# Down projections of a two-layer trunk: the block sums of the activations made one pair at a time, in place, eight units ahead; one weight sum written over the loaded block

## What is computed

```python
D_MODEL = 2048; SEQ = 256; DEPTH = 2
D_FF = 11 * D_MODEL // 4                     # 5632

def conv_glu_ffn(h, w_up, conv_w, conv_b, w_down):
    gu = h @ w_up
    gate, up = jnp.split(gu, 2, axis=-1)
    gate = causal_depthwise_conv(gate, conv_w, conv_b)
    return (jax.nn.silu(gate) * up) @ w_down

def reference(x, ...):
    for i in range(DEPTH):
        ...                                   # token mixer
        h = rms_norm(x, ffn_norm[i])
        x = x + conv_glu_ffn(h, ffn_w_up[i], ffn_conv_w[i], ffn_conv_b[i], ffn_w_down[i])
    return x
```

## Time and profile before

| | |
|---|---|
| median of 3 runs | 2106.0 us |
| lowest and highest | 2105.87 and 2107.36 us |
| the profiled execution | 2106.89 us, of which 2105.1 us is the span of the trace |
| mean granted TensorE clock | 0.997 of full |
| down stage of layer 0, from its first matmul | 893.61 us of the span |
| down stage of layer 1, from its first matmul | 1861.41 us of the span |
| busy, of the span | PE 99%, PEld 84%, DVE 67%, ACT 50%, POOL 0% |

### The profile page before, as it was taken

The page is one execution under the profiler, slowest core; times in us unless marked ns, Lnnn a source line. Parts: engine busy times, 40 slices in busy tenths (PEclk is TensorE's granted clock), DMA queues, the critical chain, the costliest instruction groups (busy, mean ns, idle before and its releaser), DMA issues.

```text
span 2105.1 us, 29925 instructions
## 1 busy us (share of the span) xinstructions
PE 2085.9 (99%) x10866; PEld 1778.5 (84%) x10866; DVE 1419.4 (67%) x1692; ACT 1048.1 (50%) x1353; POOL 0.7 (0%) x5
## 2 busy tenths in 40 slices
PE   9999999999999999999999999999999999999999
PEld 8888888888888888878888877888888888878887
DVE  5664565566676676686885677566676666687884
ACT  6554554544444444444554666554444444444553
POOL 0000000000000000000000000000000000000000
PEclk9999999999999999999999999999999999999999
DMA  7665555655655565556666544565565565556665
GB/s 251 208 180 170 165 176 172 188 173 186 191 192 185 189 199 176 189 171 203 201 208 184 181 145 135 179 185 171 194 198 173 188 198 195 178 164 210 194 210 167
DMA packets 206266, 390.69 MB, mean 186 GB/s; under 512 B 12860, under 2 KB 17772, under 8 KB 206188
## 3 DMA queue, kind: packets, MB, share of 16 engines
q1 hardware_dynamic: 203884, 387.45, 58.2%
q10 hardware_dynamic: 2304, 2.20, 0.3%
HBM read 387.48 MB, written 2.11 MB: 185 GB/s over the span
## 4 chain that ended last, share of the span: by engine, by line
PE 93%; DVE 4%; ACT 1%; DMA 1%; issue 1%; DVEq 0%; ACTq 0%
PE ps L1301 39%; PE ps L1291 31%; PE ps L1297 16%; PE ps L1316 2%; PE ps L1318 2%; PE ps L1317 2%; DVE wlo L946 1%; PE ps L1439 1%; DMA raw<-in_ffn_w_down 1%; DVE tlo L944 0%; ACT thi L658 0%; PE ps L1491 0%; PE ps L1502 0%; PE ps L1519 0%; DVE xf L1029 0%
## 5 line engine op out<-in xcount | busy, mean ns | idle before, releaser
L1291 PE MATMUL ps<-hs,whi 128*128 128x512 f32 x2832 | 663.6, 390 | 0.0
L1291 PEld LDWEIGHTS ps<-hs,whi 128*128 128x128 f32 x2832 | 524.7, 188 | 104.3
L990 DVE TENSOR_TENSOR wlo<-raw,whi 128x1024 fp32r<-128x1024 f32 x352 | 414.5, 1220 | 288.2 <-PE ps L1297 202.8
L946 DVE TENSOR_TENSOR wlo<-raw,whi 128x1024 fp32r<-128x1024 f32 x352 | 426.1, 1222 | 255.9 <-ACT whi L660 254.9
L660 ACT ACTIVATE whi<-raw 128x1024 fp32r<-128x1024 f32 x354 | 373.3, 1059 | 373.6 <-PE ps L1301 325.1
L667 ACT ACTIVATE whi<-raw 128x1024 fp32r<-128x1024 f32 x352 | 366.0, 1056 | 265.3 <-DMA raw<-in_ffn_w_up 201.6
L1297 PEld LDWEIGHTS ps<-hs,wlo 128*128 128x128 f32 x2816 | 352.6, 191 | 8.8
L1297 PE MATMUL ps<-hs,wlo 128*128 128x256 f32 x2816 | 355.3, 283 | 0.0
L1301 PE MATMUL ps<-whi,hs 128*128 128x512 f32 x1088 | 276.4, 396 | 0.7 <-ACT whi L660 0.7
L1301 PE MATMUL ps<-whi,gs 128*128 128x512 f32 x1024 | 257.2, 393 | 3.2 <-ACT whi L660 3.2
L1301 PEld LDWEIGHTS ps<-whi,hs 128*128 128x128 f32 x1088 | 199.9, 188 | 40.9 <-DVE hs L1012 0.9
(11 more groups left out here) (194 smaller groups left out, 1394.9 us busy)
## 6 DMA issues: line engine op xcount, KB each, us to landing
raw<-in_ffn_w_up SPq DMA_DIRECT2D x352, 512.0 KB, 4.5
raw<-in_ffn_w_down SPq DMA_DIRECT2D x176, 512.0 KB, 4.6
raw<-in_fox_w_in SPq DMA_DIRECT2D x98, 512.0 KB, 3.9
raw<-in_swa_w_in SPq DMA_DIRECT2D x40, 512.0 KB, 3.6
raw<-in_fox_w_out SPq DMA_DIRECT2D x32, 512.0 KB, 3.8
raw<-in_swa_w_out SPq DMA_DIRECT2D x32, 512.0 KB, 3.8
xk<-in_x SPq DMA_DIRECT2D x8, 256.0 KB, 5.9
out_x<-xk SPq DMA_DIRECT2D x8, 256.0 KB, 4.8
```

The costliest lines, as they stand in the source:

```text
L946: tt(wlo[slot][:, :], raw[slot][:, :], whi[slot][:, :].bitcast(F32), ALU.subtract).then_inc(lo_ready, 1)
L990: tt(wlo[slot][:, :], raw[slot][:, :], whi[slot][:, :].bitcast(F32), ALU.subtract).then_inc(lo_ready, 1)
L1291: return pe.matmul(ps[:, bank, :], whi[slot][:, c:c + P], moving.rearrange("p h t -> p (h t)"), start=first, stop=last)
```

## The change

`tsum`, `thi` and `tlo` hold three sums instead of four. The sum B12+B22 is written over B12 in the "t" slot, and the whole "t" slot is then split as for any other unit, after the sums; the product that uses it moves ahead of the wait for `thi` and `tlo`. The activations' sums are made for one pair at a time, in a buffer of four blocks that lies over `sqj`, each in place of what it was made from: "xc" eight places ahead of the pair (place 1 for the first), "xs" two places after that. The number of matmuls stays.

```diff
@@ -103,6 +103,7 @@
 LAST_OF = [max(i for i, s in enumerate(DOWN_ORDER) if s[:2] == ("d", g)) for g in range(4)]
+FIRST_SEVEN = [DOWN_ORDER.index(("s", 0, k)) for k in SEVEN_K]
 LAST_SEVEN = [max(i for i, s in enumerate(DOWN_ORDER) if s[:2] == ("t", c)) for c in range(2)]
...
@@ -175,12 +177,11 @@
         tsum_at = hs_at + SEVEN * 3 * 2 * P * 4
-        tsum = sb("tsum", [P, 4, 512], at=tsum_at)
-        thi = sb("thi", [P, 4, 512], F32R, at=tsum_at + 8192)
-        tlo = sb("tlo", [P, 4, 512], F32R, at=tsum_at + 16384)
-        xf = sb("xf", [P, SEVEN, 2, T], at=tsum_at)
-        xc = sb("xc", [P, SEVEN, 4, P], at=tsum_at + SEVEN * 2 * T * 4)
-        assert tsum_at + 24576 <= place[0]
+        tsum = sb("tsum", [P, 3, 512], at=tsum_at)
+        thi = sb("thi", [P, 3, 512], F32R, at=tsum_at + 6144)
+        tlo = sb("tlo", [P, 3, 512], F32R, at=tsum_at + 12288)
+        xf = sb("xf", [P, 4, P], at=sqj_at)
+        assert tsum_at + 18432 <= place[0]
         place[0] += -place[0] % 512
...
@@ -474,7 +474,9 @@
                 u = base + i
-                steps += {0: [("xf", layer)], 1: [("xc", layer)], 2: [("xs", layer)]}.get(i, [])
+                for r in range(SEVEN):
+                    at = i - max(1, FIRST_SEVEN[r] - 8)
+                    steps += {0: [("xc", layer, r)], 2: [("xs", layer, r)]}.get(at, [])
                 for c in range(2):
...
@@ -651,13 +653,13 @@
                 if kind == "t":
-                    act.activation(whi[slot][:, 512:1024], raw[slot][:, 512:1024], ACT.Copy).then_inc(hi_ready, 1)
                     act.wait_ge(v_t, 4 * m + 4)
+                act.activation(whi[slot][:, :], raw[slot][:, :], ACT.Copy).then_inc(hi_ready, 1)
+                if kind == "t":
+                    act.wait_ge(v_glo, UP_GROUPS * (m // (2 * SEVEN) + 1) + 1)
                     if m:
                         act.wait_ge(v_tl, m)
                     act.activation(thi[:, :, :], tsum[:, :, :], ACT.Copy).then_inc(a_th, 1)
-                    return
-                act.activation(whi[slot][:, :], raw[slot][:, :], ACT.Copy).then_inc(hi_ready, 1)
 
...
@@ -677,6 +679,8 @@
                     act.wait_ge(f_rd, 2 * FOX_GROUPS)
+                if n == 2:
+                    act.wait_ge(v_xs, SEVEN)
                 for t in range(TT):
...
@@ -715,9 +719,10 @@
                 elif kind == "xs":
-                    act.wait_ge(v_xc, 4 * n + 4)
-                    act.activation(xs[:, :, :, 0, :], xc[:, :, 0:3, :], ACT.Copy)
-                    act.activation(gs[:, 0:SEVEN, 0, 0, P:T], xc[:, :, 3, :], ACT.Copy).then_inc(a_xh, 1)
+                    act.wait_ge(unit_done, U_FFN[n] + 16 * UP_GROUPS)
+                    act.wait_ge(v_xc, 5 * (SEVEN * n + s[2] + 1))
+                    act.activation(xs[:, s[2], :, 0, :], xf[:, 0:3, :], ACT.Copy)
+                    act.activation(gs[:, s[2], 0, 0, P:T], xf[:, 3, :], ACT.Copy).then_inc(a_xh, 1)
                 elif kind == "rcol":
...
@@ -937,13 +942,10 @@
                     seven_sums(u, m)
+                tt(wlo[slot][:, :], raw[slot][:, :], whi[slot][:, :].bitcast(F32), ALU.subtract).then_inc(lo_ready, 1)
                 if kind == "t":
-                    half = slice(512, 1024)
-                    tt(wlo[slot][:, half], raw[slot][:, half], whi[slot][:, half].bitcast(F32), ALU.subtract).then_inc(lo_ready, 1)
                     dve.wait_ge(a_th, m + 1)
                     tt(tlo[:, :, :], tsum[:, :, :], thi[:, :, :].bitcast(F32), ALU.subtract).then_inc(v_tl, 1)
-                    return
-                tt(wlo[slot][:, :], raw[slot][:, :], whi[slot][:, :].bitcast(F32), ALU.subtract).then_inc(lo_ready, 1)
 
...
@@ -952,15 +954,18 @@
                 dve.wait_ge(w_land[(u + 1) % RAW], 16 * ((u + 1) // RAW + 1))
+                if m % (2 * SEVEN) == 0:
+                    dve.wait_ge(unit_done, U_FFN[m // (2 * SEVEN)] + 16 * UP_GROUPS)
+                    dve.wait_ge(v_glo, UP_GROUPS * (m // (2 * SEVEN) + 1) + 1)
                 if m:
                     dve.wait_ge(v_tl, m)
                     dve.wait_ge(v_e, 7 * (m // SEVEN))
                 tt(tsum[:, 0, :], b11, b12, ALU.add).then_inc(v_t, 1)
-                tt(tsum[:, 1, :], b12, b22, ALU.add).then_inc(v_t, 1)
                 dve.wait_ge(v_t, 4 * m + 1)
-                tt(tsum[:, 2, :], tsum[:, 0, :], b22, ALU.add).then_inc(v_t, 1)
+                tt(b12, b12, b22, ALU.add).then_inc(v_t, 1)
+                tt(tsum[:, 1, :], tsum[:, 0, :], b22, ALU.add).then_inc(v_t, 1)
                 dve.wait_ge(v_t, 4 * m + 3)
-                tt(tsum[:, 3, :], tsum[:, 2, :], b21, ALU.add).then_inc(v_t, 1)
+                tt(tsum[:, 2, :], tsum[:, 1, :], b21, ALU.add).then_inc(v_t, 1)
 
...
@@ -1022,25 +1027,27 @@
                     seven_out(n, s[2], s[3], s[4])
-                elif kind == "xf":
-                    dve.wait_ge(unit_done, U_FFN[n] + 16 * UP_GROUPS)
-                    dve.wait_ge(v_glo, UP_GROUPS * (n + 1) + 1)
-                    part = lambda h: gs[:, 0:SEVEN, 0:2, h, :].bitcast(F32)
-                    tt(xf[:, :, :, :], part(0), part(1), ALU.add).then_inc(v_xf, 1)
                 elif kind == "xc":
-                    a11, a21, a12, a22 = (xf[:, :, f, t * P:t * P + P] for f in range(2) for t in range(TT))
-                    n1, s3, s4, s1 = (xc[:, :, i, :] for i in range(4))
-                    dve.wait_ge(v_xf, n + 1)
-                    tt(s1, a21, a22, ALU.subtract).then_inc(v_xc, 1)
-                    tt(s3, a11, a21, ALU.subtract).then_inc(v_xc, 1)
-                    dve.wait_ge(v_xc, 4 * n + 1)
-                    tt(n1, a11, s1, ALU.subtract).then_inc(v_xc, 1)
-                    dve.wait_ge(v_xc, 4 * n + 3)
-                    tt(s4, a12, n1, ALU.subtract).then_inc(v_xc, 1)
+                    x0, e0 = SEVEN * n + s[2], 5 * (SEVEN * n + s[2])
+                    n1, s3, s4, s1 = (xf[:, i, :] for i in range(4))
+                    part = lambda h: gs[:, s[2], 0:2, h, :].bitcast(F32)
+                    dve.wait_ge(v_glo, UP_GROUPS * n + s[2] + 2)
+                    dve.wait_ge(a_ss, 8 * n + 8)
+                    if x0:
+                        dve.wait_ge(v_xs, x0)
+                    tt(xf[:, :, :].rearrange("p (f t) c -> p f (t c)", t=TT), part(0), part(1), ALU.add).then_inc(v_xc, 1)
+                    dve.wait_ge(v_xc, e0 + 1)
+                    tt(s1, s3, s1, ALU.subtract).then_inc(v_xc, 1)
+                    dve.wait_ge(v_xc, e0 + 2)
+                    tt(s3, n1, s3, ALU.subtract).then_inc(v_xc, 1)
+                    dve.wait_ge(v_xc, e0 + 3)
+                    tt(n1, n1, s1, ALU.subtract).then_inc(v_xc, 1)
+                    dve.wait_ge(v_xc, e0 + 4)
+                    tt(s4, s4, n1, ALU.subtract).then_inc(v_xc, 1)
                 elif kind == "xs":
-                    dve.wait_ge(a_xh, n + 1)
-                    tt(xs[:, :, :, 1, :], xc[:, :, 0:3, :], xs[:, :, :, 0, :].bitcast(F32), ALU.subtract)
-                    tt(gs[:, 0:SEVEN, 0, 1, P:T], xc[:, :, 3, :], gs[:, 0:SEVEN, 0, 0, P:T].bitcast(F32), ALU.subtract).then_inc(v_xs, 1)
+                    dve.wait_ge(a_xh, SEVEN * n + s[2] + 1)
+                    tt(xs[:, s[2], :, 1, :], xf[:, 0:3, :], xs[:, s[2], :, 0, :].bitcast(F32), ALU.subtract)
+                    tt(gs[:, s[2], 0, 1, P:T], xf[:, 3, :], gs[:, s[2], 0, 0, P:T].bitcast(F32), ALU.subtract).then_inc(v_xs, 1)
                 elif kind == "prep":
...
@@ -1320,8 +1327,9 @@
                 if kind == "s":
+                    if c == 0:
+                        pe.wait_ge(v_xs, SEVEN * layer + i + 1)
                     if first:
-                        pe.wait_ge(v_xs, layer + 1)
                         pe.wait_ge(v_up, UP_GROUPS * (layer + 1) + 1)
...
@@ -1329,12 +1337,12 @@
                 product(2, mixed(2), w(whi, 1), w(wlo, 1), False, False)
+                product(7, mixed(1), w(whi, 0), w(wlo, 0), first, last)
                 pe.wait_ge(a_th, m + 1)
                 pe.wait_ge(v_tl, m + 1)
                 product(5, act_in(0, 1), sums(thi, 0), sums(tlo, 0), first, last)
-                product(7, mixed(1), sums(thi, 1), sums(tlo, 1), first, last)
-                product(6, mixed(0), sums(thi, 2), sums(tlo, 2), first, last)
-                product(1, act_in(1, 1), sums(thi, 3), sums(tlo, 3), False, False).then_inc(unit_done, 1)
+                product(6, mixed(0), sums(thi, 1), sums(tlo, 1), first, last)
+                product(1, act_in(1, 1), sums(thi, 2), sums(tlo, 2), False, False).then_inc(unit_done, 1)
 
...
```

More of the change, by code:

```diff
@@ L165, in trunk @@
         ssum = sb("ssum", [P, TT])
+        sqj_at = place[0]
         sqj = sb("sqj", [P, TT, 512])
@@ L352, in trunk @@
         v_out = sem("v_out")
-        v_xf = sem("v_xf")
         v_xc = sem("v_xc")
```

## The result

| | median | lowest and highest | runs |
|---|---|---|---|
| before | 2106.55 us | 2105.87 to 2107.68 | 10 |
| after | 2111.77 us | 2109.79 to 2115.00 | 10 |

After stands to before as 1.0026, with a 95% interval from 1.0017 to 1.0036: about 5 us slower, where 6.4 us less were forecast. The measured time lies 0.8 us over the top of the range. The profiled execution took 2111.71 us, of which 2109.9 us is the span, 4.8 more than before.

The account below looks back on a forecast made before the run. PE, busy 99% of the span, was taken as the bound; per layer 0.2 + 5 x 1.07 = 5.55 us lost, against 8.7 and 8.8, gains 6.4: 2099.6 us median, range 2094.5 to 2111.

Parts of the forecast that it names:

- the most to be won: PE's loss near the start of the two down stages, 8.7 and 8.8 us, 17.5 us in all.
- The start: From a down stage's first matmul to its first pair: loss shrinks from 8.7 to 0.2 us, clock doesn't fall.
- The chain of a pair: From the start of a pair's sums to the end of `tlo`: 6.95 us after the change, 6.90 before.
- "xc" in the loop: The next pair's "xc" on DVE, between `tlo` and two low parts: 2.0 us, between 1.7 and 2.4.
- the loop: Half 0, beside PE: `tlo`, "xc", two low parts, next "t" load's landing, next sums; 16.7 us against PE's 15.64.
- The landing: The next pair's "t" load in half 0 lands 5.2 us after issue, 4.7 to 5.6 in the forecast.
- The sum: Loss per layer 5.55 us after, against 8.7 and 8.8: gain 6.4 us, 2100.5 profiled, 2099.6 median.
- (a): Rival: the "t" load keeps its landing, mean 6.2; period 17.7, 3.5 us slower in all, 2109.5; chance 0.22.
- Half 1: After half 0: no stops before; the later `whi` of "t" costs 0.05, the extra product gives 0.68 us.
- (b): Rival: landings of 6.8, three loads sharing the queue in every pair; period 18.3, 9.5 us slower, 2115.5; chance 0.12.
- (d): Rival: PE's stop of about 1 us at each pair lets its clock fall, 2104 to 2109; chance 0.09.
- (c): Rival: the loop keeps up and all 17.5 us come back, 2088.5; needs a landing of 4.1 or less; chance 0.05.

Follow-up runs that it names:

- the first run: The changed kernel with "xc" and "xs" of pairs 1 to 5 moved later, "xc" behind the two low parts: 2092.17 us, 0.9934 of before.

## Why the prediction was wrong

**What bounds the kernel, and the most to be won: right.** The 17.5 us were the stage's loss. With "xc" behind the low parts 14.4 come back; the place of that loss and its cause (DVE busy with six blocks at once) were as described.

**The start: right.** 918.69 - 894.08 leaves 0.1 us of loss in layer 0, where 0.2 was forecast, and the clock stays at 1.00. In layer 1 it is 1889.57 - 1864.16 = 25.4, 0.9 of loss, 0.7 more than forecast.

**The chain of a pair: nearly right.** From the sums to the start of `tlo` 934.64 - 929.30 = 5.34, then 1.76: 7.10, where 6.95 was forecast. The second sum now waits for the first (0.73 behind it instead of 0.60), which gives the missing 0.15.

**"xc" in the loop: right.** From 918.46 to 920.37 it is 1.91 us; 2.0 was forecast. It stands where it was said to stand, and the two low parts behind it are 2.35.

**The landing: wrong, and this is the step that failed.** I took 5.2 us, because the queue would be empty at the first load of the pair and because the nearest row seemed to be the load at 893.4. The queue was empty as forecast, or nearly: the load in front had landed, or landed within 0.15 us, in nine of the ten pairs, and in all of them by the time of the "t" load. The third load followed after 1.8 us (1.95 forecast). My "nothing in front" was misread: the load at 893.4 is the second of two, 1.1 us behind its first, which is the changed kernel's pattern in front; but its third was 2.3 us behind. These are its neighbours in the trace of before:

```profile
L566 SPq DMA_DIRECT2D raw<-in_ffn_w_down x1: 368/368/368, 892.3 to 892.3; - x1
...
L566 SPq DMA_DIRECT2D raw<-in_ffn_w_down x1: 368/368/368, 895.7 to 895.7; - x1
...
L566 SPq DMA_DIRECT2D raw<-in_ffn_w_down x1: 368/368/368, 896.8 to 896.8; - x1
...
DMA to landing us min/median/max: 6.0/6.0/6.0
```

The rows with a third at 1.8 us or less were the 6.4 and 6.8 of the earlier trace rows. I explained these by two things at once, the third load and loads of an earlier step that still ran; in these rows they can't be told apart, as both stand in each. The changed kernel has the third load without the earlier ones and still took 6.1, and the run with the later third load takes it down to 5.2. Loads in front may cost as much: the one at 896.8 has three within 4.6 us in front and none behind for 9.6 us, and took 6.0. In the changed kernel the load at this place took 5.1, so one row alone can be off by a us, and my 5.2 rested on one. The landing measured 6.08 in the mean of the ten pairs. The 0.88 over 5.2, ten times, is 8.8 us.

**The sum.** Forecast for the span: 2105.1 - 6.4 = 2098.7; measured 2109.9, 11.2 more. The ten periods took 175.3 us against 167.1: 8.2 us, in which the 8.8 of the landing and 1.5 of the chain are partly offset by a cheaper "xc" and by hand-overs of 0.2 instead of 0.3. The starts give 0.7. Some 2.3 lie where I had expected nothing: 0.9 in the pairs of half 1 in layer 0, 0.7 at the end of that half, 0.5 before the stage of layer 0, and the rest between the halves. The 0.7 is for the most part a wait of PE for `xk`, to which DVE adds the stage's results, of 0.87 us where it was 0.26. The run with "xc" behind the low parts has it too (0.95). In the medians the miss is 2111.77 - 2099.6 = 12.2 us, 1.0 more than in the span: I had set the median 0.9 below the profiled execution, as before, but after they are equal. A slip of 0.5 stands in the range: (a) with "xc" at 2.2 is 2109.5 + 2 = 2111.5, not 2111, and the measured time lies over that too.

**Half 1: wrong in a small way.** I had said that the later `whi` of "t" costs 0.05 there. In half 1 of layer 0 the pairs stand 10.3, 10.2, 10.5, 10.5 and 10.5 us apart, 52.0 in all, where PE needs 10.20 and the kernel before took 51.1; in layer 1 all are at 10.20. The run with the weights' half alone takes 51.8 there, with one period of 10.9, and the two with the activations' half alone take 51.1. So the loss comes with the weights' half, and it fits a low part of "t" that now stands behind the sums and so frees its slot later. But the run with "xc" behind the low parts has the weights' half too and takes 51.0, and layer 1 has the same order and no loss. Why only some of them lose it stays open.

**The rivals.** The one that happened is (a), the landing stays as it is: 6.08 with a mean period of 17.5, against its 6.2 and 17.7. In part this is luck: before, the third load stood 1.1 us behind and the load in front of the group 3.7, after it is 1.8 and 5.0, and nothing shows that these had to give the same landing. Its time of 2109.5 is 2.3 us under the measured one: the losses in the other places and at the starts are 3.0, the shorter period takes 1.7 back, and the rest is the 0.9 of the median. I gave it 0.22. It got less than it deserved because I refuted a rule and took that for evidence against (a): the Trainium skill, "DMA: Bandwidth & Descriptors", section "Queues, rings and completion order", says that each DMA engine takes descriptors in ring order. I concluded that by that rule a third load can't delay a second, so that the landing would stay, and set the rows with a close third load against it. The same section says that data descriptors carry no barrier, so that a later one may finish its write first; and by the traces a later load does cost the one in front of it (6.4 against 5.2 us with 1.1 us more between them). Row and page were at odds only by my reading, and the row decides. But the same rows spoke for (a) and not against it: from "a third load close behind slows the second" I should have gone on to "and the changed kernel has one close behind", 1.95 us by my own count, where the 6.4 of the earlier trace rows had it at 1.8. The decision point of (b), a period of 17.35 or a landing of 5.8, was well placed: 6.08 is over it, and the kernel is slower. (d) did not happen: stops of 1.2 to 1.7 us at eight of the ten pairs left the clock at 1.00. (c) needed a landing of 4.1 in the order of the change, and is not what the better order does: that one takes "xc" out of the loop.

## What to carry to other kernels

When work is spread out in time, the question isn't whether the engine has time for it, but which release it now stands in front of: the same 1.9 us of DVE's time per pair cost 18.6 us of half 0 in the two layers ahead of two low parts, against the same work behind them, where half 0 runs within 0.3 us of PE's own time. A landing isn't a constant of a load: read it from rows with the same loads in front and behind, at the same distances, since where the load belongs to a loop each tenth of a us is paid in every period. And if an engine is idle before a step that is said to be late, first look for the transfer that it waits for and for what released that.

## What the runs showed of the hardware

- The landing of one 512 KB load depends on what is issued behind it as well as in front of it: 3.7 us alone; with one 1.1 us in front and the next 2.9 behind, 4.9 to 5.5; with one 1.1 in front and the next 1.8 behind, 6.2 to 6.7 in eight of ten cases, and 6.0 to 6.6 in all ten of the run with the activations' half alone; with one 3.0 in front and the next 1.9 behind, 3.9 to 4.8. The first load of the group, with the second 1.1 us behind, took 3.8 to 4.4 in the changed kernel.
- The load before the group may count as well: in the first run, where the group's first load was issued 3.0 us behind it, that first load took 4.6 to 6.3 and the "t" load 4.9 to 6.4, though the third was 3.0 behind. No run changes this distance alone.
- Twice in ten the close pattern took only 4.5 and 5.0, with issues at the same distances (939.5, 940.6 and 942.4 us for the 4.5). Nothing in the traces tells these two from the others; that stays open.
- Stops of PE of up to 1.7 us, one or two per 17.5 us, did not lower the granted clock, though two stops of 1.7 and 1.6 us within 5 us of each other had stood in a stretch with 0.93.
